# Two-block hybrid-attention program: the index scores of block 1 one product sooner, top-k rounds and a memory half ahead of the attention's step 0, and other slots for the memory halves

## The reference, cut to what matters

```python
h = x @ w_in
qa, ka, va, qb, kb, vb, qi, ki, wi = jnp.split(h, cuts, axis=-1)
...
sc = jnp.einsum('bqhd,bsd->bqhs', qib, ki)                 # 8 index heads of 32
idx_score = jnp.einsum('bqhs,bqh->bqs', jax.nn.relu(sc), wib)
idx_score = jnp.where(causal[None], idx_score, NEG)
_, sel = lax.top_k(idx_score, k_top)                       # k_top = 64
...
mix = jnp.concatenate([oa, ob], axis=-1) @ w_o
x = layer_norm(DN_ALPHA * x + mix, ln1_g, ln1_b)
```

## Time and profile before

| | |
|---|---|
| device time, median of three runs | 1554.95 us (1549.97 to 1555.04) |
| profiled execution, span from first to last instruction | 1552.6 us |
| PE busy | 1497.1 us (96%) |
| DVE busy | 1062.8 us (68%) |
| ACT busy | 778.0 us (50%) |
| POOL busy | 123.2 us (8%) |
| mean granted TensorE clock | 0.990 |
| layer 0 of block 1: first attention scores to first product with w_o | 71.64 to 118.41 us |
| layer 1 of block 1: the same | 402.17 to 451.72 us |

### The profile page before, as it was taken

The page is one execution under the profiler, slowest core; times in us unless marked ns, Lnnn a source line. Parts: engine busy times, 40 slices in busy tenths (PEclk is TensorE's granted clock), DMA queues, the critical chain, the costliest instruction groups (busy, mean ns, idle before and its releaser), DMA issues.

```text
span 1552.6 us, 21682 instructions
## 1 busy us (share of the span) xinstructions
PE 1497.1 (96%) x8433; PEld 1264.8 (81%) x8433; DVE 1062.8 (68%) x1713; ACT 778.0 (50%) x1162; POOL 123.2 (8%) x98
## 2 busy tenths in 40 slices
PE   8999999999899999999999999999999999999997
PEld 5877888888677888878877988888788779888886
DVE  7777587667766787676345566878863555677777
ACT  4563544444554444434565344666545653446563
POOL 0130000000210000011022000000010320000000
PEclk9999999999999999999999999999999999999999
DMA  7534655656235655644614745556536147345551
GB/s 260 196 101 138 217 190 190 212 172 209 93 119 172 235 190 190 226 157 135 193 56 152 252 134 172 185 190 216 176 121 195 54 151 257 126 168 184 189 190 66
DMA packets 184429, 265.03 MB, mean 171 GB/s; under 512 B 7368, under 2 KB 139398, under 8 KB 184200
## 3 DMA queue, kind: packets, MB, share of 16 engines
q1 hardware_dynamic: 178712, 258.38, 50.2%
q10 hardware_dynamic: 5616, 5.26, 1.0%
HBM read 258.38 MB, written 5.24 MB: 170 GB/s over the span
## 4 chain that ended last, share of the span: by engine, by line
PE 77%; DVE 13%; ACT 4%; issue 3%; DVEq 2%; POOL 1%; ACTq 0%; POOLq 0%; DMA 0%; SPq 0%
PE psw L815 18%; PE psw L814 8%; PE psw L742 8%; PE psw L744 7%; PE psw L743 7%; DVE wlo L1735 5%; PE psa L742 4%; PE psa L744 4%; PE psa L743 4%; PE psa L876 3%; PE psa L874 3%; PE psa L926 2%; PE psw L898 2%; PE psa L943 1%; PE psw L818 1%
## 5 line engine op out<-in xcount | busy, mean ns | idle before, releaser
L1735 DVE TENSOR_TENSOR wlo<-raw,whi 128x2048 fp32r<-128x2048 f32 (+3 forms) x199 | 449.9, 2266 | 124.5 <-ACT whi L1347 124.1
L815 PE MATMUL psw<-xboth,whi 128*128 128x512 f32 x1344 | 464.7, 396 | 1.2 <-DVE wlo L1735 1.2
L1347 ACT ACTIVATE whi<-raw 128x2048 fp32r<-128x2048 f32 (+3 forms) x199 | 375.0, 1885 | 175.6 <-PE psw L744 91.3
L814 PE MATMUL psw<-xboth,wlo 128*128 128x256 f32 x1176 | 327.9, 279 | 0.0
L815 PEld LDWEIGHTS psw<-xboth,whi 128*128 128x128 f32 x1344 | 242.7, 188 | 49.1 <-DVE wlo L1735 2.3
L814 PEld LDWEIGHTS psw<-xboth,wlo 128*128 128x128 f32 x1176 | 221.7, 189 | 7.5
L742 PE MATMUL psw<-whi,xboth 128*128 128x512 f32 (+3 forms) x472 | 181.8, 385 | 6.4 <-DVE wlo L1735 5.3
L744 PE MATMUL psw<-whi,xboth 128*128 128x512 f32 (+3 forms) x472 | 178.8, 379 | 0.0
L743 PE MATMUL psw<-wlo,xboth 128*128 128x512 f32 (+3 forms) x472 | 178.6, 378 | 0.0
L1409 ACT ACTIVATE r<-psw 128x512 f32<-128x512 f32 x88 | 52.5, 596 | 174.7 <-PE psw L815 164.2
L742 PE MATMUL psa<-whi,rr 128*128 128x512 f32 x352 | 137.5, 391 | 1.4 <-DVE rr L2365 1.3
(11 more groups left out here) (290 smaller groups left out, 2209.9 us busy)
## 6 DMA issues: line engine op xcount, KB each, us to landing
raw<-in_w_gu SPq DMA_DIRECT2D x44, 1024.0 KB, 5.1
raw<-in_ffn_w_up SPq DMA_DIRECT2D x42, 1024.0 KB, 5.1
raw<-in_w_down SPq DMA_DIRECT2D x22, 1024.0 KB, 4.9
raw<-in_ffn_w_down SPq DMA_DIRECT2D x22, 1024.0 KB, 4.8
raw<-in_w_in SPq DMA_DIRECT2D x20, 1024.0 KB, 5.3
raw<-in_xa_wkv SPq DMA_DIRECT2D x16, 1024.0 KB, 5.4
raw<-in_w_o SPq DMA_DIRECT2D x8, 1024.0 KB, 5.2
raw<-in_w_out SPq DMA_DIRECT2D x8, 1024.0 KB, 5.2
```

What stands on the lines that cost most here:

```text
L814: pe.matmul(bank[:, 0:S], wl[:, k, cols], xhi[:, k, :], start=False, stop=False)
L815: ins = pe.matmul(bank.rearrange("p (i s) -> p i s", i=2), wh[:, k, cols], xboth[:, :, k, :], start=k == 0, stop=k == KD - 1)
L1347: nc.scalar.activation(tile_flat("hi", i), tile_flat("raw", i), ACT.Copy).then_inc(hi_ready, 1)
L1735: v.tensor_tensor(tile_flat("lo", i), tile_flat("raw", i), tile_flat("hi", i).bitcast(F32), ALU.subtract).then_inc(lo_ready, 1)
```

## The change

- `index_scores(0)` goes ahead of piece (5, 1) and `index_scores(1)` ahead of piece (6, 0). The ReLU of tile 1 has a buffer of its own (`cblocks`), and `icomb_done` is gone.
- On DVE `index_sum(1)` follows `index_sum(0)` directly, ahead of the rotary embedding of the last heads. Four top-k rounds of tile 0 run ahead of step 0; the rest are spread 2, 2 with the mask, 2, 2, 2, 2 with the mask.
- Head turns: groups 6 and 7 go to banks 0 and 1 of `psa`, so that they wait for no eviction. The first memory half stands between groups 4 and 5.
- `SLOTS1` becomes (0, 1, 2, 4, 6, 8), where slot 0 stands for the half done ahead of step 0. The half of step 2 uses bank 2 of `psa`; the first value products wait until it has been copied out.

```diff
-SLOTS1 = (1, 2, 3, 5, 7, 9)
+SLOTS1 = (0, 1, 2, 4, 6, 8)
+HALF_BANKS1 = (3, 3, 2, 3, 3, 3)
+TOP_FIRST = 4
+TOP_STEPS = {0: (0, 4, 6), 1: (0, 6, 8), 2: (1, 0, 2), 3: (1, 2, 4), 4: (1, 4, 6), 5: (1, 6, 8)}
...
-        relu = sy[:, 1, :].rearrange("p (h k) -> p h k", h=H)
+        relus = [sy[:, 1, :].rearrange("p (h k) -> p h k", h=H), cblocks[:, 0:2048].rearrange("p (h k) -> p h k", h=H)]
...
+        head_banks = [(psa, 0), (psa, 1), (psw, 0), (psw, 2), (psw, 1), (psw, 3), (psa, 0), (psa, 1)]
...
+            def half_in_attention(l, n):
+                q = n - FIRST_HALF[1, l]
+                bank = HALF_BANKS1[q]
+                earlier = [p for p in range(q) if HALF_BANKS1[p] == bank]
+                if earlier:
+                    pe.wait_ge(kv_staged, FIRST_HALF[1, l] + earlier[-1] + 1)
+                memory_half(n, psa[:, bank, 0:TC])
...
+                        if block == 1 and n == first:
+                            pe.wait_ge(kv_staged, FIRST_HALF[1, l] + HALF_BANKS1.index(2) + 1)
...
-                             (6, 0): first_scores})
-                pe.wait_ge(relu_done, NT * l + 1)
-                index_scores(1)
+                             (5, 1): first_scores, (6, 0): second_scores})
+
+                pe.wait_ge(qkb_roped, NT * (l + 1))
+                for q in range(2, 5):
+                    pe.wait_ge(proj_ready, 8 * l + q + 3)
+                    head_turns(q)
+                pe.wait_ge(relu_done, NT * (l + 1))
+                memory_half(FIRST_HALF[1, l])
                 pe.wait_ge(proj_ready, 8 * (l + 1))
...
+                for q in range(5, 8):
                     head_turns(q)
...
                 for q in range(2, 8):
                     heads_out(q)
+                    if q == 4:
+                        memory_store(FIRST_HALF[1, l], stage[0][:, 0, :])
...
                     if q == 5:
                         index_sum(0)
+                        index_sum(1)
...
                 serve((1, "in", l, 6))
-                index_sum(1)
-                dve.drain()
+                top_rounds(0, 0, TOP_FIRST)
```

More of the change, by code:

```diff
@@ L903, in attention @@
                     n = memory_slot(block, l, i - first)
-                    if n is not None:
-                        if n:
-                            pe.wait_ge(kv_staged, n)
+                    if n is not None and block == 1 and i > first:
+                        half_in_attention(l, n)
+                    if n is not None and block == 2:
+                        pe.wait_ge(kv_staged, n)
                         memory_half(n)
@@ L1026, in head_turns @@
                 def head_turns(q):
+                    bank, place = head_banks[q]
                     for j, b in enumerate(head_groups[q]):
                         for t in range(NT):
-                            ins = pe.transpose((psa if q < 2 else psw)[:, q % 4, j * S + t * P:j * S + (t + 1) * P],
+                            ins = pe.transpose(bank[:, place, j * S + t * P:j * S + (t + 1) * P],
                                                roped[:, t, b * P:(b + 1) * P], ident[:])
@@ L1456, in attention @@
                     half = memory_slot(block, l, i - first)
-                    if half is not None:
-                        memory_store(half, stage[block - 1][:, half % 2, :])
+                    if half is not None and block == 1 and i > first:
+                        memory_store(half, stage[0][:, half % 2, :],
+                                     psa[:, HALF_BANKS1[half - FIRST_HALF[1, l]], 0:TC])
+                    if half is not None and block == 2:
+                        memory_store(half, stage[1][:, half % 2, :])
                     if first <= i - 2 < first + count:
@@ L1508, in heads_out @@
                     nc.scalar.activation(headT[:, grp[0]:grp[0] + nb, :],
[L1509 removed]
+                                         bank2(*head_banks[q])[:, 0:nb, :], ACT.Copy).then_inc(heads_ready, 1)
                 def rectified(t):
@@ L2029, in index_sum, with top_rounds @@
                     for h in range(H):
-                        ins = v.scalar_tensor_tensor(out=sc, in0=relu[:, h, 0:nk], scalar=wi_s[:, t, h:h + 1],
-                                                     in1=cm if h == 0 else sc, op0=ALU.mult, op1=ALU.add)
-                        if h < H - 1:
-                            dve.drain()
-                    ins.then_inc(icomb_done, 1)
+                        v.scalar_tensor_tensor(out=sc, in0=relus[t][:, h, 0:nk], scalar=wi_s[:, t, h:h + 1],
+                                               in1=cm if h == 0 else sc, op0=ALU.mult, op1=ALU.add)
+                        dve.drain()
+                def top_rounds(t, r0, r1):
+                    nk = (t + 1) * P
+                    sc = iscore[:, t, 0:nk]
+                    for _ in range(r0, r1):
+                        v.max(out=top8[:], in_=sc)
+                        dve.drain()
+                        v.match_replace(out=sc, in_to_replace=top8[:], in_values=sc, imm_value=TAKEN)
+                        dve.drain()
+                    if r1 == TOPK // 8:
+                        v.tensor_scalar(dmask[:, t, 0:nk], sc, TAKEN / 2, MASKED, ALU.is_gt, ALU.mult)
+                        dve.drain()
+                        v.tensor_tensor(dmask[:, t, 0:nk], dmask[:, t, 0:nk], causal[:, S - nk:S], ALU.add)
+                        dve.drain()
                 t1 = sy[:, 0, 0:640]
@@ L2098, in _ @@
                 serve((1, "in", l, 6))
-                index_sum(1)
-                dve.drain()
+                top_rounds(0, 0, TOP_FIRST)
                 def top(step):
[L2104 to L2118, removed]
+                    if step in TOP_STEPS:
+                        top_rounds(*TOP_STEPS[step])
                 def mask(kind, h, t):
```

25 lines of the change are left out of this document (9 added, 16 removed).

## The result

The changed kernel takes 1564.96 us (median of four runs, 1563.11 to 1566.01), the kernel before 1554.64 (1549.97 to 1555.04). The ratio is 1.0074, with a 95% interval of 1.0055 to 1.0093: slower, by 10 us, which is clear of the interval and under 1%. The profiled execution has a span of 1564.2 where the kernel before had 1552.6, so 11.6 us are to be found in the traces.

The account below looks back on a forecast made before the run. PE, busy 96% of the span, was taken as the bound. Leads of 1.7 and 2.3 us, 4.7 more per layer and 4 for clock falls made +9.4 on 1552.6, a median of 1564, range 1555 to 1571.

Parts of the forecast that it names:

- Ahead of P0: Up to P0, the value product of half unit 0: it comes 1.7 us sooner in layer 0, 2.3 in layer 1.
- full behind the head turns: Sign on PE's granted clock: full behind the head turns, at 0.5 behind two or three of the gaps.
- Rounds hidden in layer 0: DVE in layer 0: four top-k rounds end about 73.7, ahead of the first scores' end at 74.75, so are hidden.
- From P0 on: From half unit 0's value product to the first w_o product: 33.7 us instead of 29.04, 4.7 more in each layer.
- The clock: PE clock falls behind the new gaps: two to three, 4 us, between 0 and about 10.
- The sum: Whole kernel: layer 0 +3.0, layer 1 +2.4, together +5.4; with clock falls +9.4 on the span, median 1564.
- rival 1: PE's gaps come as forecast in both layers but the clock holds: +5.4 us, 1560; chance 0.33.
- rival 2: No loss behind P0, since PE's queue and ACT's store overlap better; only leads stay: -4.0 us, 1551; chance 0.07.
- Rival 3: Front worse too: GpSimd's rotary work beside layer 0's index sums, late rotary in layer 1: +4 us, 1568; chance 0.10.

Follow-up runs that it names:

- e11: Changed kernel with ACT's store of the last three memory halves put behind the copies to pt of its step; 1558.4 us, ratio 1.0031.
- e12: e6 with the fourth half of layer 1 in step 4 instead of 5 and its store behind the copies to pt; 1551.9 us, ratio 0.9994.
- e3: e1 with the sixteen top-k rounds spread as in the kernel before, none ahead of step 0; 1557.7 us, ratio 1.0033.
- e5: Changed kernel with matmuls of no use filling PE's waits without being meant to prolong them; results not read; 1561.3 us, ratio 1.0048.
- e2: Kernel before with only its last three memory halves of each layer moved from steps 5, 7, 9 to 4, 6, 8; 1567.2 us, ratio 1.0093.
- e1: Changed kernel with its last three memory halves of each layer back in steps 5, 7 and 9; 1554.8 us, ratio 1.0008.
- e6: e1 with the second tile's two top-k rounds taken from step 2 and spread over steps 3 to 5; 1550.6 us, ratio 0.9984.
- e9: e6 with the second index sum behind the last rotary work in layer 1 only; 1552.9 us, ratio 1.0000.
- e10: e8 with the second index sum of layer 0 ahead of the last rotary work again; 1556.0 us, ratio 1.0022.
- e8: Changed kernel with later halves in steps 1, 3, 5, 7, 9, top-k rounds later, second index sum behind the last rotary work; 1562.2 us, ratio 1.0055.

## Why the prediction held, step by step

- **Ahead of P0.** First scores at 73.74 (predicted 74.05), P0 at 87.16 behind 2.39 (87.7 behind 2.5). Right. In layer 1 the lead is 1.9 (2.3), but the wait ahead of P0 is 0.60 and not 2.9: the turns waited 2.05 for the rotary work as predicted, and then the clock was low over the scores (2.08) and the half (5.61), which made PE late instead of idle. I had counted the new stretch at the full clock, and the forecast's sign "full behind the head turns" failed here. Most of it cost nothing at P0, since ACT was the later one anyway, but not all: in e11 and e12 the clock is full over these scores (1.16), P0 waits the predicted 2.87 and 2.88, and from the first scores to P0 it is 13.90 instead of 14.43. This fall cost 0.5.
- **Rounds hidden in layer 0.** The timeline of DVE in the changed kernel, layer 0 and 1, against the earlier trace rows:

```profile
73.62 0.28 DVE L2062 MATCH_REPLACE8 r<-top,r 128x128 f32<-128x128 f32 x1
74.50 0.29 DVE L1842 CUSTOM_DVE_ANT_0 sy<-psw,band 128x128 f32<-128x128 f32 x1 [0.60 <-PE psw L910]
...
414.33 0.28 DVE L2062 MATCH_REPLACE8 r<-top,r 128x128 f32<-128x128 f32 x1
415.08 0.29 DVE L1842 CUSTOM_DVE_ANT_0 sy<-psw,band 128x128 f32<-128x128 f32 x1 [0.48 <-PE psw L910]
```

  The last of the four rounds is done while PE still works on the first scores: DVE then waits 0.60 and 0.48 for them. That the four rounds are more than hidden, and worth 2.9 us against the old spread, I had not seen; e3 showed it.
- **From P0 on.** 33.7 was predicted with the clock full. The changed kernel has falls in both layers, but the pieces at the full clock are all there. In its layer 1, P0 to P1 takes 5.47, to P2 4.80, to P3 6.76, to P4 5.17, and P5 to w_o 7.14; P4 to P5 takes 4.64 in e11. The sum is 34.0, so 4.9 more than 29.04 in each layer, against the 4.7 predicted, and e5 has 34.0 and 34.1 with the waits filled. (e11's 33.8 and 33.7 agree by accident: its waits are 1.7 shorter, and one fall makes up for it.) The waits ahead of P2, P4 and P6 are 2.41, 2.42 and 1.59 (2.4, 2.3, 1.5 predicted), all ended by the copy to pt, none ahead of P1, P3, P5. This is the main term, and e2 shows that it comes from the steps alone. e11 confirms the store as 0.8 of each wait.
- **The clock.** This term was mis-sized: two to three falls, 4 us, against four behind P0, 38.7 + 35.6 - 2 x 34.0 = 6.3 us by the trace, 1.6 each, and 6.1 by e5. The price of one was right and their number too low; how many fall the forecast could only guess.
- **The sum.** Predicted -4.0 + 9.4 + 4 = +9.4 on the span; measured -2.2 - 1.9 (leads) + 9.9 (waits) + 6.3 (clock) = +12.1 at w_o of layer 1, where the trace has 463.79 - 451.72 = 12.1. The rest of the program gave 0.5 back. The span moved by 11.6 and the median by 10.3; the profiled run took 1566.0, 1.0 above its median. So the mechanism held, the sum was 2.7 too low at w_o, and that the median came within 1 us of the 1564 forecast is in part luck.
- **Rivals.** The clock did not hold, which rules out rival 1; rival 2 needed ACT to take under 2.3 us from P1's end to P2, and it took 4.1 (94.92 to 99.00). Rival 3's slower index sum is real (below), but hidden: DVE still waits 0.60 for the first scores. Of its layer 1 there is only the 2.05 that the forecast had.

The rule of the Trainium skill that I weighed (TensorE: Matmul & The Clock Gate, "HAM oscillation — how this bites in real kernels") describes a kernel that returns to the low clock at the wait of every tile, and gives these waits as about 3 to 5 us. Here shorter ones did it, and not every one: of the eight waits of 2.41 to 2.46 ahead of P2 and P4 in the changed kernel and e2, six were followed by a low clock; the two that were not are the waits of 2.46 ahead of P2 in layer 1.

## What to carry to other kernels

In an in-order pipeline of two engines, filler work belongs between what the other engine is waiting for and what it will deliver, and not ahead of the instruction that it waits for: one step's difference cost 10 us here. (Where that instruction has to wait anyway, the place is free: in layer 1 of e12 a half in step 4 took the place of P1's wait of 2.33 and lost nothing.) A lead won at the front counts only if the next product's own chain (here the fourth maximum) is early as well, so follow the second and third consumer, not only the first. And a store of a result that nobody needs soon goes behind the copy that somebody waits for.

## What the runs showed of the hardware

- A low clock follows some waits of one length and not others. Ahead of P0 in layer 0 the wait was 2.39 or 2.40 in the changed kernel, e1, e11 and e12, with the granted clock down to 0.50 behind it, and in e6 and e9, where it stayed full. Behind the nine waits of 1.58 to 1.61 ahead of P2, P4 or P6 (changed kernel, e2, e11, e12) it never fell. Ahead of P5 in layer 0 a wait of 1.95 had a fall behind it in e10 and none in e8. No run shows what decides it.
- The rest of the program, which no edit touches, took 1097.0 (e5) to 1105.1 us (e9) from w_o of layer 1 on. In e5 the clock falls there at 697 and 1366, in e9 at 701, 776 and 1206, and near the very end in both. Executions of one kernel differ by as much (e9's twelve runs lie between 1551.1 and 1557.5, e5's ten between 1557.7 and 1565.3, and the traced ones are the 1557.5 and the 1557.7), so these traces do not show it as an effect of the edits. It is more than several of the edits are worth, so the stretch is read from the trace and the time from the runs.
- The vector engine's seven steps of the first index sum took 4.21 us in layer 0, with GpSimd at its rotary work from 57.03 to 61.21, and 2.95 in layer 1, where GpSimd did nothing from 400.07 to 402.75. The whole difference lies beside GpSimd's work: the two steps that start before 61.21 take 0.67 and 1.33, the five behind them 0.35 each, as in layer 1. The smaller pieces of GpSimd from 402.75 on slow them little. Timeline of DVE and then of POOL in the changed kernel:

```profile
59.29 4.21 DVE L2051 SCALAR_TENSOR_TENSOR r<-sy,wi_s,r 128x128 f32<-128x128 f32 x7
...
401.35 2.95 DVE L2051 SCALAR_TENSOR_TENSOR r<-sy,wi_s,r 128x128 f32<-128x128 f32 x7
```

```profile
59.95 1.26 POOL L2446 TENSOR_TENSOR r<-pt 128x512 f32<-128x512 f32 x1
```
